# The w_in product of k and v in seven block products, with the mixer pieces moved behind it

## What is computed

```
proj = rmsnorm(x) @ w_in                    # 2048 x (512 + 512 + 1024 + 1024 + 16 + 3*512 + 2*512)
q, k, v, r, a_lr, cb, cc, ch, cu, cv = split(proj)
loga = log_sigmoid(a_lr @ w_a2 + b_a) / 16
o    = gated linear attention(q, k, v, loga, state)      # chunks of 64, 4 heads
o_gla = rmsnorm(o) * gla_g * silu(r)
o_conv = cb * (short convolution of cc * ch)
o_cm = gelu(cu) * (causal 128x128 mix of layernorm(gelu(cv)))
h = x + concat(o_gla, o_conv, o_cm) @ w_out
y = rmsnorm(h + swiglu(rmsnorm(h)))
```

## Time and profile before

| | us |
|---|---|
| median of 3 runs | 2218.58 (2217.26 to 2219.17) |
| profiled execution | 2217.63 |
| its span | 2215.9 |
| TensorE busy in the span | 2199.1 |
| VectorE busy | 1656.6 |
| ScalarE busy | 970.4 |

### The profile page before, as it was taken

One profiled execution on the slowest core, in us unless ns is written; L12 is line 12 of the kernel. 1 busy time (PEld: TensorE's weight loads), 2 busy tenths in 40 slices (PEclk: granted clock), 3 DMA queues, 4 the chain that ended last, 5 costly groups with the idle time before them and its releaser, 6 DMA issues.

```text
span 2215.9 us, 41279 instructions
## 1 busy us (share of the span) xinstructions
PE 2199.1 (99%) x17457; PEld 2191.0 (99%) x17457; DVE 1656.6 (75%) x1922; ACT 970.4 (44%) x1267; POOL 10.1 (0%) x16
## 2 busy tenths in 40 slices
PE   9999999999999999999999999999999999999997
PEld 9999999999999999999999999999999999999997
DVE  7346544447496688887887887888888888788787
ACT  6334222113254454444544444444444545444454
POOL 0000000000000000000000000000000000000000
PEclk9999999999999999999999999999999999999998
DMA  5222242444323425445435434444545786455522
GB/s 196 86 77 77 78 153 94 145 142 151 104 86 105 155 107 170 142 133 162 141 128 164 150 120 152 156 136 139 163 142 167 279 292 221 177 206 189 193 96 100
DMA packets 122698, 325.49 MB, mean 147 GB/s; under 512 B 10603, under 2 KB 55211, under 8 KB 121548
## 3 DMA queue, kind: packets, MB, share of 16 engines
q1 hardware_dynamic: 122044, 323.69, 43.4%
q10 hardware_dynamic: 528, 0.07, 0.0%
HBM read 267.09 MB, written 56.63 MB: 146 GB/s over the span
## 4 chain that ended last, share of the span: by engine, by line
PE 98%; ACT 1%; issue 0%; DVE 0%; DMA 0%; POOLq 0%; POOL 0%; SPq 0%; DVEq 0%; ACTq 0%
PE acc L1325 36%; PE acc L1085 28%; PE g L1325 27%; PE acc L1274 2%; PE g L1274 2%; PE g L1225 0%; PE g L1112 0%; PE g L1211 0%; PE g L1217 0%; PE g L1126 0%; PE g L1214 0%; PE g L1174 0%; PE g L1164 0%; DMA tmp<-w_alr 0%; PE g L1246 0%
## 5 line engine op out<-in xcount | busy, mean ns | idle before, releaser
L906 ACT CAST w_hi<-w_s 128x1024 fp32r<-128x1024 f32 (+1 forms) x204 | 209.5, 1027 | 360.1 <-DVE w_s L1983 352.3
L1085 PE MATMUL acc<-op_hi,w_hi 128*128 128x272 f32 x1664 | 347.7, 290 | 1.3 <-DVE w_lo L1476 1.3
L1085 PE MATMUL acc<-op_hi,w_lo 128*128 128x272 f32 x1664 | 344.4, 288 | 0.0
L1085 PE MATMUL acc<-op_lo,w_hi 128*128 128x272 f32 x1664 | 343.1, 288 | 0.0
L1325 PE MATMUL g<-op_hi,w_hi 128*128 128x272 f32 x1056 | 306.2, 290 | 0.0
L1325 PE MATMUL g<-op_hi,w_lo 128*128 128x272 f32 x1056 | 306.1, 290 | 0.0
L1325 PE MATMUL acc<-op_hi,w_hi 128*128 128x272 f32 x1056 | 305.8, 290 | 0.2 <-ACT acc L882 0.2
L1325 PE MATMUL acc<-sg_hi,w_hi 128*128 128x272 f32 x1056 | 305.9, 290 | 0.0
L1325 PE MATMUL acc<-op_hi,w_lo 128*128 128x272 f32 x1056 | 305.6, 289 | 0.0
L1325 PE MATMUL acc<-sg_hi,w_lo 128*128 128x272 f32 x1056 | 305.6, 289 | 0.0
L1325 PE MATMUL g<-op_lo,w_hi 128*128 128x272 f32 x1056 | 304.4, 288 | 0.0
(11 more groups left out here) (318 smaller groups left out, 4536.2 us busy)
## 6 DMA issues: line engine op xcount, KB each, us to landing
w_raw<-w_in SPq DMA_DIRECT2D x88, 512.0 KB, 3.4
w<-w_gu SPq DMA_DIRECT2D x88, 512.0 KB, 3.3
w_raw<-w_gu SPq DMA_DIRECT2D x88, 512.0 KB, 3.9
hf_dram<-hf_hi SPq DMA_DIRECT2D x22, 952.0 KB, 6.5
hf_dram<-hf_lo SPq DMA_DIRECT2D x22, 952.0 KB, 8.8
w_raw<-w_d SPq DMA_DIRECT2D x32, 512.0 KB, 4.6
w<-w_d SPq DMA_DIRECT2D x32, 512.0 KB, 3.3
op_hi<-hf_dram SPq DMA_DIRECT2D x16, 544.0 KB, 6.8
```

Source lines behind the costliest of these rows:

```text
L906: nc.scalar.copy(w_hi[:, (C_ST + n) % RING, 0:w], src[:, 0:w]).then_inc(hi_ready, 1)
L1085: last = nc.tensor.matmul(acc[t % 2][:, a, 0:TH], w, x[:, k, a * TH:(a + 1) * TH], start=start and n == 0, stop=stop and n == 2)
```

## The change

K and v, twelve column tiles, leave the scheme of chunks. For the first 12 of the 16 K tiles they are computed in six slots (`NQ`), one for two column tiles, by seven products (`Q_ORDER`) of six weight tiles (`HQ`) and 272 columns: 18 matmuls each. The remaining four K tiles are one block per slot of 48 matmuls (`None` in `Q_ORDER`) that adds into the same four banks. A slot needs four weight blocks of 384 KB and one of 512 KB, four sums of weight blocks on VectorE (`kv_sum`), eight splits, bank copies on ScalarE and five output instructions on VectorE (`kv_outputs`).

The forms of x that the products need (`th`, `tl`: differences of its half tiles, split) are made while q is computed: twelve multiplications of x by the gain on ScalarE between the squares, three times three subtractions (`t_made_kv`), three casts (`t_hi_kv`) and three differences (`t_lo_kv`).

The order is now: `a_lr` and q (chunks to 9, `C_Q` = 10), the six slots, then cv, the convolution, cu and r in 56 chunks from `C_T` = 58 on. `var1` stands behind chunk 8; all other pieces stand behind chunks of these 56. v is transposed in three pieces in place of eight, with the same 40 transposes. Buffers move: the gelu sums get their own `lnb`, the squares of cm go to `cmq`, `qm` and `vs4` share a place. The small constants `wa2`, `wm` and `bs` are loaded later in the SyncE queue, and the reload of x is issued at C_T + 50 of `C_OUT` = C_T + 56; before, it was at 76 of 90.

```diff
-T_Q, T_K, T_CV, T_CU, T_V, T_CONV, T_R, N_IN = 1, 5, 9, 13, 17, 25, 37, 45
+T_Q, T_CV, T_CONV, T_CU, T_R, N_IN = 1, 17, 21, 33, 37, 45
 HK = KT // 2
 CH = HK * P
 RING = 4
 RAW = 2
-C_OUT = 2 * N_IN
+NP = 7
+NQ = 6
+HQ = 6
+Q_ORDER = (0, 1, 2, 3, 4, None, 5, 6)
+NPQ = len(Q_ORDER)
+C_Q = 10
+C_T = C_Q + NPQ * NQ
+C_OUT = C_T + 2 * (N_IN - T_CV)
 MIX_SINGLE_AT = C_OUT - 6
...
-VAR1_AT = 6
-Z_AT = (8, 11)
-B_AT = (19, 21, 23, 25, 27)
-KDT_AT = 29
-MU_AT, VAR_CM_AT, VVT_AT, ZC_AT = 28, 31, 34, (36, 38)
-VT_AT = tuple(37 + 2 * i for i in range(8))
-P_AT = (53, 57, 61, 65)
-QS_AT = tuple(42 + i for i in range(8))
-S_AT = tuple(50 + 2 * i for i in range(10))
-OSQ_AT = 69
-ON_AT = (71, 73, 75, 77)
+GROUPS = ((0, 2), (2, 4), (4, 6))
+VAR1_AT = 8
+VT_AT = tuple(C_T + i for i in range(3))
+Z_AT = (C_T + 3, C_T + 6)
+B_AT = tuple(C_T + 8 + 2 * i for i in range(5))
+KDT_AT = C_T + 18
+QS_AT = tuple(C_T + 21 + i for i in range(8))
+MU_AT, VAR_CM_AT, VVT_AT, ZC_AT = C_T + 20, C_T + 23, C_T + 30, (C_T + 31, C_T + 32)
+S_AT = (C_T + 29, C_T + 30) + tuple(C_T + 31 + 2 * i for i in range(8))
+P_AT = tuple(C_T + 34 + 2 * i for i in range(4))
+OSQ_AT = C_T + 40
+ON_AT = tuple(C_T + 42 + 2 * i for i in range(4))
...
+                if k < 2 * HQ:
+                    act.wait_ge(op_rdy, k + 1)
+                    nc.scalar.mul(trunk[:, k, :], trunk[:, k, :], vec[:, V_G1 + k:V_G1 + k + 1]).then_inc(x_scaled, 1)
                 if k == HK:
                     split_hi(6, 6)
                     act.wait_ge(chunk_done, 4)
                     early(alr[0:2 * RANK, :], g23[0:2 * RANK, :, 0:TH])
-                    early(qT[:, 0, :], accv(1))
+                    early(q_first, accv(1))
+                if k in (7, 11):
+                    t_hi_kv(k // 4 - 1)
 
...
+            def kv_block_hi(s, pos):
+
+                n, side, idx = NPQ * s + pos, slice(s % 2, s % 2 + 1), Q_ORDER[pos]
+                act.wait_ge(chunk_done, done_q(n - 4))
+                if pos == 0 and s:
+                    seed_d_kv(s - 1)
+                if pos == 4:
+                    if s == 0:
+                        act.wait_ge(acc_free, 5)
+                    bank_read_kv(s, C22)
+                    nc.scalar.copy(pb[:, side, 0:TH], pa[:, side, 0:TH]).then_inc(seeded_kv, 1)
+                if pos == 5:
+                    bank_read_kv(s, C12)
+                    if s == 0:
+                        act.wait_ge(sq_add, KT)
+                    nc.scalar.copy(aside[:, side, 1, :], pc[:, side, 0:TH]).then_inc(p5_kv, 1)
+                if pos == 6:
+                    nc.scalar.copy(aside[:, side, 0, :], pb[:, side, 0:TH]).then_inc(u2_kv, 1)
+                if idx is None:
+                    act.wait_ge(blk_kv_in[4], 16 * (s + 1))
+                    nc.scalar.copy(w_hi[:, slot_kv(n), :], kv_c[:]).then_inc(hi_ready, 1)
+                    return
+                if idx in (0, 3, 6):
+                    act.wait_ge(blk_kv_in[(0, 0, 0, 3, 0, 0, 2)[idx]], 16 * (s + 1))
+                else:
+                    act.wait_ge(s_kv_made, 4 * s + (0, 1, 2, 0, 3, 4, 0)[idx])
+                nc.scalar.copy(w_hi[:, slot_kv(n), 0:HQ * P], block_kv(idx)).then_inc(hi_ready, 1)
+
...
+            for c in range(3, C_Q):
+                act.wait_ge(chunk_done, c + 1)
+                if c in (5, 7, 9):
+                    act.wait_ge(kvt_rdy, 1)
+                    early(qT[:, c // 2 - 1, :], accv(c // 2))
+                if c == 3:
+                    split_hi(7, 7)
+                    t_hi_kv(2)
+                elif c < 6:
+                    split_hi(c + 4, c + 4)
+                for kind, i in plan.get(c, ()):
+                    post(kind, i)
+                if c >= 6:
...
-                if kind == "qs" and before[-1][0] == "vt":
-                    before = before[:-1]
+                if kind == "qs" and i:
+                    before = order[:number(("qs", i - 1))]
...
+            def kv_product(s, pos):
+                n, side, idx = NPQ * s + pos, s % 2, Q_ORDER[pos]
+                slot = slot_kv(n)
+                pe.wait_ge(hi_ready, C_Q + n - 1)
+                pe.wait_ge(lo_ready, C_Q + n - 1)
+                if idx is None:
+                    for bank, m, a in ((pa, 0, 0), (pc, 0, 1), (pb, 1, 1), (pd, 1, 0)):
+                        if bank is pc:
+                            pe.wait_ge(p5_kv, s + 1)
+                        if bank is pb:
+                            pe.wait_ge(seeded_d_kv, s + 1)
+                        for j in range(KT - 2 * HQ):
+                            at, k = (m * (KT - 2 * HQ) + j) * P, 2 * HQ + j
+                            w_h, w_l = w_hi[:, slot, at:at + P], w_lo[:, slot, at:at + P]
+                            x_h, x_l = op_hi[:, k, a * TH:(a + 1) * TH], op_lo[:, k, a * TH:(a + 1) * TH]
+                            for i, (w, x) in enumerate(((w_h, x_h), (w_h, x_l), (w_l, x_h))):
+                                last = nc.tensor.matmul(bank[:, side, 0:TH], w, x, start=False,
+                                                        stop=j == KT - 2 * HQ - 1 and i == 2, skip_group_check=True)
+                    last.then_inc(chunk_done, 1)
+                    return
+                for j in range(HQ):
+                    w_h, w_l = w_hi[:, slot, j * P:(j + 1) * P], w_lo[:, slot, j * P:(j + 1) * P]
+                    x_h, x_l = rhs_kv(idx, j)
+                    for i, (w, x) in enumerate(((w_h, x_h), (w_h, x_l), (w_l, x_h))):
+                        last = nc.tensor.matmul(banks[idx][:, side, 0:TH], w, x, start=idx < 2 and j == 0 and i == 0,
+                                                stop=j == HQ - 1 and i == 2, skip_group_check=True)
+                last.then_inc(chunk_done, 1)
+
+            for c in range(4, C_Q):
+                tile_half(c)
+            for s in range(NQ):
+                for pos in range(NPQ):
+                    if pos == 0 and s < 2:
+                        pe.wait_ge(acc_free, 4)
+                    elif pos == 0:
+                        pe.wait_ge(kv_read, 4 * (s - 2) + C11 + 1)
+                    elif pos == 1 and s < 2:
+                        pe.wait_ge(post_a, 1)
+                    elif pos == 1:
+                        pe.wait_ge(kv_read, 4 * (s - 2) + C12 + 1)
+                    elif pos == 2:
+                        pe.wait_ge(seeded_kv, s + 1)
+                    elif pos == 4:
+                        pe.wait_ge(u2_kv, s + 1)
+                    if s == 0 and pos == 1:
+                        pe.wait_ge(kvt_rdy, 3)
+                    kv_product(s, pos)
+            for c in range(C_T, C_OUT):
+                tile_half(c)
...
+            def t_made_kv(i):
+
+                at, end = GROUPS[i]
+                b = xg[:, at:end]
+                dve.wait_ge(x_scaled, 2 * end)
+                nc.vector.tensor_tensor(b[:, :, 0:2, :], b[:, :, 1::2, :], b[:, :, 0:2, :], ALU.subtract)\
+                    .then_inc(kvt_made, 1)
+                dve.wait_ge(kvt_made, 3 * i + 1)
+                nc.vector.tensor_tensor(b[:, :, 3, :], b[:, :, 3, :], b[:, :, 0, :], ALU.subtract).then_inc(kvt_made, 1)
+                dve.wait_ge(kvt_made, 3 * i + 2)
+                nc.vector.tensor_tensor(b[:, :, 2, :], b[:, :, 2, :], b[:, :, 3, :], ALU.subtract).then_inc(kvt_made, 1)
+
+            def t_lo_kv(i):
+
+                at, end = GROUPS[i]
+                dve.wait_ge(kvt_h, i + 1)
+                nc.vector.tensor_tensor(tl[:, :, at:end, :], xg[:, at:end, :, :].rearrange("p i b t -> p b i t"),
+                                        f32(th[:, :, at:end, :]), ALU.subtract).then_inc(kvt_rdy, 1)
+
             for k in range(KT):
...
+                if k == 5:
+                    t_made_kv(0)
+                if k == 9:
+                    t_lo_kv(0)
+                    t_made_kv(1)
+                if k == 13:
+                    t_lo_kv(1)
+            t_made_kv(2)
...
+            for c in range(3, C_Q):
+                dve.wait_ge(chunk_done, c + 1)
+                if c < 6:
+                    split_lo(c + 4, c + 4)
+                if c == 3:
+                    t_lo_kv(2)
+                if c == 6:
+                    kv_sum(0, 0)
+                if c >= 6:
+                    kv_block_lo(0, c - 6)
+                if c == 7:
+                    kv_sum(0, 1)
+                    kv_sum(0, 2)
+                for kind, i in plan.get(c, ()):
+                    post(kind, i)
+            for s in range(NQ):
+                for pos in range(NPQ):
...
```

More of the change, by code:

```diff
@@ L97 @@
 V_G1, V_G2, V_GF, V_GLA, V_CW, V_CB, V_LG, V_LB, NV = 0, 16, 32, 48, 56, 68, 72, 76, 80
-A_KINDS = ("var1", "z", "b", "mu", "var_cm", "vvt", "p", "s", "on")
-V_KINDS = A_KINDS + ("kdt", "zc", "vt", "qs")
+A_KINDS = ("var1", "vt", "z", "b", "mu", "var_cm", "vvt", "p", "s", "on")
+V_KINDS = A_KINDS + ("kdt", "zc", "qs")
 def mixer_plan():
@@ L114, in mixer_plan, with tile_of @@
     return plan, order
+def tile_of(c):
```

(57 more changed lines are left out.)

355 lines of the change are left out of this document (255 added, 100 removed).

## The result

| | before | after |
|---|---|---|
| median of 4 runs | 2218.47 (2217.26 to 2219.17) | 2240.27 (2237.10 to 2243.27) |
| profiled execution | 2217.63 | 2239.72 |
| its span | 2215.9 | 2238.0 |
| mean granted TensorE clock | 0.997 | 0.991 |

The ratio is 1.0099, 95% interval 1.0081 to 1.0116: slower by 1.0%, 21.8 us, where 15.4 us were forecast. Times are in microseconds. A line number is that of the kernel whose profile is shown, so one and the same line of code can be L1085 before, L1261 in the changed kernel and L1266 in a run.

The account below looks back on a forecast made before the run. TensorE, busy 2199.1 of 2215.9 us, was taken as the bound. From 2218.6, work -12.6, start +12.0, `qs` 3 +5.2, clock +1.5 twice, short stalls +1.9, +2.5, +3.4: +15.4, so 2234; range 2226 to 2241.

Parts of the forecast that it names:

- TensorE's work: K and v columns: six slots of 174 matmuls, 131.7 us, replace 24 chunks, 144.3 us; gain 12.6 us.
- The start: In q, before chunk 7: TensorE stands 12.0 us because split_lo(7) comes behind the new forms on VectorE; 7.2 to 13.
- `qs` 3: At C_T + 23: VectorE does a conv tile, then var_cm, so TensorE stalls 5.2 us.
- `s` 1, `s` 2, `s` 8, `s` 9: Mixer pieces now too close behind vvt, zc 0, on 0 and on 1: stalls of 1.9, 2.5 and twice 1.7 us.
- The clock: Behind the stalls before chunk 7 and qs 3: some 3.2 us at half pace lose about 1.5 us each.
- The argument against this, that full chunks lie on both sides of them: Against falls behind short stalls: around the old 2.41 us wait matmuls had one column, here full chunks lie on both sides.
- The rival with four more falls: The clock falls after the short stalls too, four more falls at 1.45 us: 2240; chance 0.10.
- The slots: Six k and v slots: VectorE's 14 us fit in 21.9, so they cost nothing; if not, 1.5 us a slot.
- the clock rival with a start wait of 13: High end of the range: falls after the short stalls too, with a 13 us stall before chunk 7; 2241.

Follow-up runs that it names:

- Run 2: Changed kernel with the splits of chunks 7, 8 and 9 ahead of the second and third group of forms, nothing left out; 2232.07 us, ratio 1.0062.
- Run 6: Changed kernel with b pieces one chunk up, mu at C_T + 16, var_cm at C_T + 18 (even), kdt at C_T + 20; 2236.03 us.
- runs 3: Changed kernel with a looser plan: mu, var_cm, b, qs, s 0 and s 1 earlier, kdt and zc one chunk later; 2235.24 us, ratio 1.0076.
- run 11: Changed kernel with reordered start, var_cm moved, zc one and on two chunks down, plus matmuls of ones before s 1, s 3, s 9; 2221.30 us.
- run 12: Changed kernel with reordered start, var_cm moved, zc one chunk down, plus matmuls of ones before s 1, s 3, s 8, s 9; 2215.72 us.
- runs 1 and 4: Changed kernel with, first, only chunk 7's split ahead of the second forms, 2244.12 us; second, 92 and 44 matmuls of ones before chunk 7 and qs 3, 2253.36 us.

## Why the prediction was right and where not

The direction was right, and so were the mechanism and the places of the waits: a slower kernel, with the predicted waits before chunk 7, `qs` 3, `s` 1, `s` 2, `s` 8 and `s` 9 and no other of a microsecond or more. What the waits do to the clock was put too low. The sum was 6.4 us short.

- *TensorE's work* was to give 12.6; it gave 13.2. A slot takes 21.85 and not 21.94.
- *The start*, 12.0, measured 10.7 and 10.5, and 7.7 to 10.1 in three more kernels with the forms ahead of the splits. Run 2, which changes the order alone and has no wait, shows that the order causes it.
- *`qs` 3*, 5.2, measured 5.3. Run 6 shows that the place of `var_cm` causes it; that the conv tile ahead of it is the reason is the prediction's sum (4.9 of the 13.2 us on VectorE) and fits runs 3 and 6, but no run changes the tile alone.
- *`s` 1, `s` 2, `s` 8, `s` 9*: 1.9, 2.5, 1.7, 1.7; measured 2.0, 2.6, 1.9, 1.9. All waits together were put at 25.0 and came to 24.4.
- *The clock is the term that failed in size*: "some 3.2 us at half pace lose about 1.5 us", counted twice, 3.0. It came to 8.5 (7.9 without the slower first matmuls). Behind the long waits a fall costs more than behind the one of 2.41 us that the trace of before had (2.45 and 2.65), and it came behind two of the four short waits as well. The argument against this, that full chunks lie on both sides of them, does not hold: it was drawn from one case of another kind. The rival with four more falls, 2240, is the nearest of the cases; two of its four were there, behind `s` 1 and `s` 2, at about the size it had.
- *The Trainium skill* ("TensorE: Matmul & The Clock Gate", the section on the HAM clock gate) says that the throttled clock is the default and that activity releases it. The traces agree at the two long waits: wherever they were not filled the clock fell (5 profiles in 5 before chunk 7 or 8, 4 in 4 before `qs` 3). The Trainium skill's advice (same title, "HAM oscillation") is on idle gaps longer than the short waits here, so by it these would have cost no clock; the measurement decides, and it has falls behind waits as short as 1.2 us (3 times in 3 before `s` 3), though not behind each of them (6 times in 6 not, before `qs` 0).
- *The slots*: none starved.
- *Not in the sum*: about 2 us of the last stages.

For the two profiles the terms close: 5.5 more for the clock, 2.0 in the last stages and 0.4 that is in none of the terms, less 0.6 for the slots and 0.6 for the waits, make 6.7; the spans differ by 22.1 where 15.4 was forecast.

The time of 2240.27 is within the range of 2226 to 2241, but not by the forecast of 2234: the upper end came from the clock rival with a start wait of 13. That it lies within 1 us of that rival's 2240 is partly luck, since two of the rival's four falls did not come in the profile, and the long waits' dearer falls and the last stages filled their place.

## What to carry to other kernels

Where one engine is busy for 99% of the time, moving work costs at the places where another engine's queue has new work ahead of what the first one waits for. Follow each queue instruction by instruction; that gave each of six waits within 1.3 us here. Then count the clock behind every wait of TensorE: nothing, or some 1.5 to 1.7 us a time behind a wait of 1 to 3 us (now and then twice that), and about 2.5 behind the waits of 5 and 10 us here. A wait that can't be removed can be filled with matmuls that no one reads, a little shorter than the wait (5.1 us gained in run 11, 9 in run 12). Before a plan of pieces is squeezed from 90 chunks into 56, look which chunks VectorE has other work in: `var_cm` cost a wait of 5.3 us on an odd chunk with a `qs` right behind it, 1.0 and 2.7 on an odd one further ahead, and 1.2 on an even one as far ahead.

## What the runs showed of the hardware that was not expected

**A fall has nearly a fixed price, and the length of the wait does not decide whether it comes.** The loss of a fall is the time at a clock of 0.50, times a half. Behind the short waits of the mixer pieces it is 0.00 or 1.71, and twice 3.41 (behind `s` 1 in runs 1 and 4), never between. Behind the wait of 2.1 to 2.4 us near the end, in all 14 profiles, it is 0.00 once, 1.71 nine times and 3.41 four times. Leaving out filled waits: before `s` 8 (1.9 us) 3 falls in 10 profiles; before `s` 9 (1.9) 9 in 11; before `s` 1 (2.0) 9 in 10; before `s` 2 (2.6) 8 in 8; before `s` 3 (1.2) 3 in 3; before `qs` 0 (1.2) none in 6. Windows behind the wait before `s` 8, of the changed kernel and then of run 2:

```profile
556.00:560.00 4.00, 3.56 (x28) 3.56 (x29) 3.85 (x7) 1.70 (x2) 0.00 (x0) 1.00 0.38 97
```

```profile
545.00:549.00 4.00, 3.75 (x22) 3.75 (x23) 3.85 (x7) 1.89 (x3) 0.00 (x0) 0.73 0.40 94
```

What differs besides the wait was not isolated; the places with no fall in one kernel and a fall in another have the same work around them, at other times. It also fell without any wait, at or right behind the four float32 matmuls of `z` 0 (3.6 us), in 6 of 13 profiles. The spread of up to 7.4 us between the runs of one kernel (run 11; run 12 had 3.0) fits to that: in run 11 the mean clock is 0.997 in the fastest execution and 0.994 in the slowest, and 0.003 of 2220 us is 6.7. A single profile's clock must not be taken for the kernel's.

**A float32 matmul is two instructions.** The matmuls of ones of 128 columns took 0.223 us each, two instructions of 0.112 (88 in 9.82), while those on rounded operands of 272 columns take one of 0.125.
